# A hybrid gMLP, short-convolution and expert step on one core: mixing biases as products over 128 partitions, mixing between the last blocks of u, and a plan with a turn or two between an engine's step and its readers

## What is computed

```python
def chunk_mlp_mixer(x, w_in, ln_g, ln_b, w_s, b_s, w_out):
    z = jax.nn.gelu(x @ w_in)
    u, v = jnp.split(z, 2, axis=-1)
    v = layer_norm(v, ln_g, ln_b)
    ws = jnp.where(mask[None], w_s[:, :L, :L], 0).astype(v.dtype)
    bias = jnp.transpose(b_s[:, :L]).astype(v.dtype)
    mixed = jnp.einsum('gij,bcjgd->bcigd', ws, vc) + bias[None, None, :, :, None]
    y = (u * mixed.reshape(bsz, s_len, D_A)) @ w_out
    return y, v

def peer_ffn(h, w_query, sub_keys, expert_u, expert_v):
    ...
        u_sel = expert_u[idx]
        a = jax.nn.gelu(jnp.einsum('thkd,td->thk', u_sel, xb))
        return jnp.einsum('thk,thkd->td', g.astype(a.dtype) * a, expert_v[idx])
```

## Time and profile before

| | us |
|---|---|
| median of 3 runs | 1812.18 |
| lowest, highest of the 3 | 1812.14, 3855.36 |
| the profiled execution, its time | 1814.52 |
| its span in the profile | 1812.7 |

### The profile page before, as it was taken

How to read it: one execution, slowest core, us unless ns; L and a number is a source line. 1 busy time by engine, 2 the same in 40 slices (tenths; PEclk the granted TensorE clock), 3 DMA queues, 4 the chain that set the end, 5 groups by cost and what they waited for, 6 DMA issues and landing times.

```text
span 1812.7 us, 23002 instructions
## 1 busy us (share of the span) xinstructions
PE 1370.5 (76%) x8388; PEld 648.4 (36%) x8388; DVE 1217.0 (67%) x3197; ACT 293.1 (16%) x972; POOL 689.7 (38%) x580
## 2 busy tenths in 40 slices
PE   8997899998895887876664499779965667677643
PEld 6884345554462553541110066336511111111100
DVE  1237878545685867768889666666788975555565
ACT  1112123100222111211112111021211110000011
POOL 0003343323332343334544543343344444444453
PEclk9999799969997999986765599889977666665655
DMA  9739999979999999999999999999999999999996
GB/s 381 292 141 422 358 379 422 421 278 422 421 421 421 402 421 420 417 421 413 415 413 387 422 407 409 421 421 411 421 421 414 403 421 421 421 420 416 414 421 278
DMA packets 100657, 718.27 MB, mean 396 GB/s; under 512 B 12064, under 2 KB 12576, under 8 KB 13600
## 3 DMA queue, kind: packets, MB, share of 16 engines
q0 software_dynamic: 82944, 604.02, 81.1%
q1 hardware_dynamic: 17184, 112.19, 15.1%
q10 hardware_dynamic: 416, 0.60, 0.1%
HBM read 715.24 MB, written 1.52 MB: 395 GB/s over the span
## 4 chain that ended last, share of the span: by engine, by line
DMA 48%; PE 34%; DVE 8%; issue 7%; DVEq 2%; POOL 1%; ACT 0%; SPq 0%; POOLq 0%
DMA uvring<-expert_uv_dram,idx 44%; PE psum L657 13%; PE psum L668 10%; DMA wring<-w_chunks_dram 3%; PE psum L787 3%; PE psum L700 3%; DVE uvring L1198 2%; DVE diag L1209 1%; POOL uvring L610 1%; PE psum L770 1%; PE psum L767 1%; PE psum L676 1%; PE psum L649 1%; DVEq L990 1%; PE psum L739 1%
## 5 line engine op out<-in xcount | busy, mean ns | idle before, releaser
L610 POOL DMA_INDIRECT uvring<-expert_uv_dram,idx x576 | 689.5, 1197 | 1100.8 <-PE psum L657 874.5
L1198 DVE SCALAR_TENSOR_TENSOR uvring<-uvring,xn 128x1024 f32<-128x1024 f32 x576 | 705.1, 1224 | 371.7 <-DMA uvring<-expert_uv_dram,idx 360.4
L657 PE MATMUL psum<-uvring,diag 64*64 64x512 f32 x4096 | 704.8, 775 | 311.9 <-DVE diag L1209 300.5
L657 PEld LDWEIGHTS psum<-uvring,diag 64*64 64x64 f32 x4096 | 128.0, 155 | 734.4 <-DVE diag L1209 667.9
L914 ACT ACTIVATE a_gelu<-a_raw 128x1 f32<-128x1 f32 x576 | 115.2, 202 | 1109.9 <-DVE uvring L1198 1109.1
L668 PE MATMUL psum<-xT,wring 128*128 128x160 f32 (+1 forms) x1696 | 248.1, 302 | 15.4 <-DMA wring<-w_chunks_dram 14.7
L668 PEld LDWEIGHTS psum<-xT,wring 128*128 128x128 f32 x1696 | 226.9, 198 | 91.4 <-issue 61.9
L1209 DVE TENSOR_SCALAR diag<-twin,a_gelu,gate 128x64 f32<-128x64 f32 x512 | 158.9, 310 | 24.0 <-ACT a_gelu L914 23.8
L649 PE MATMUL psum<-uvring,diag 128*32 128x256 f32 x512 | 69.0, 634 | 90.5 <-DVE diag L1209 84.6
L836 ACT ACTIVATE arena<-psum 128x160 f32<-128x160 f32 (+2 forms) x160 | 47.7, 299 | 302.2 <-PE psum L668 240.9
L787 PE MATMUL psum<-wring,arena 128*128 128x256 f32 x288 | 70.0, 399 | 5.1 <-DMA wring<-w_chunks_dram 4.8
(11 more groups left out here) (117 smaller groups left out, 849.6 us busy)
## 6 DMA issues: line engine op xcount, KB each, us to landing
wring<-w_chunks_dram SPq DMA_DIRECT2D x73, 1024.0 KB
uvring<-w_chunks_dram SPq DMA_DIRECT2D x15, 1024.0 KB, 9.4
kept<-w_chunks_dram SPq DMA_DIRECT2D x12, 1024.0 KB, 15.6
uvring<-expert_uv_dram,idx POOLq DMA_INDIRECT x576
x<-x_tok_dram SPq DMA_DIRECT2D x2, 512.0 KB, 4.2
uvring<-ln_gain_dram SPq DMA_DIRECT2D x1, 1024.0 KB, 28.2
uvring<-ln_bias_dram SPq DMA_DIRECT2D x1, 1024.0 KB, 28.6
keys<-sub_keys_dram SPq DMA_DIRECT2D x2, 512.0 KB, 8.2
```

The costliest lines, as they stand in the source:

```text
L610: pool.indirect_dma_start(uvring[:, n % RING, :], None, expert_uv, bass.IndirectOffsetOnAxis(ap=idx[t][:, i:i + 1], axis=0),).then_inc(uv_ ...
L657: mm = nc.tensor.matmul(acc[64 * j:64 * j + 64, 512 * i:512 * (i + 1)], diag[64 * i:64 * i + 64, n % DIAGS, :], row[64 * i:64 * i + 64, D ...
L1198: nc.vector.scalar_tensor_tensor(out=uvring[:, slot, 0:D], in0=uvring[:, slot, 0:D], scalar=1.0, in1=xn[t][:, :], op0=ALU.mult, op1=ALU.mu ...
```

## The change

Three things are changed.

1. The bias of tiles 0 and 1 is a product over all 128 partitions, that of tile 2 still over 32. The biases of the 8 groups stand in the rows of `bias`, and the stationary matrix is column g of the unit matrix, repeated. The table loses a row, and the constant that is loaded for `bias` grows from 4 KB to 64 KB.
2. The mixing groups stand between the last blocks of u: group b-9 behind block b from block 9 on, the rest behind block 15. The `lnb` steps begin behind block 1 and not 3.
3. `ready` asks for distance in the plan: a step may read another engine's result one turn later, and for the kinds in `slow` TensorE's two turns later. The costs of TensorE's small steps are lower, those of the blocks higher, and TensorE's room in tile (0, 0) is 2.0 and not 1.85.

```diff
-    blk, row = KD * WIDTH[n] * mm, KD * WCOLS * mm
+    blk, row = 1.14 * KD * WIDTH[n] * mm, KD * WCOLS * mm
...
-            out.append(("PE", ("vq", c), row / 2, [x_read]))
+            out.append(("PE", ("vq", c), 0.6, [x_read]))
...
-            if n == 1 and 3 <= b < 11:
-                q, a = divmod(b - 3, 2)
-                out.append(("PE", ("lnb", q, a), 0.9, []))
+            if n == 1 and 1 <= b < 9:
+                q, a = divmod(b - 1, 2)
+                out.append(("PE", ("lnb", q, a), 0.6, []))
                 out.append(("DVE", ("lnrow", q, a), 1.4, [("lnb", q, a), ("root", "ln", 0, 2)]))
+
+            for g in range(GROUPS) if b == KA - 1 else (b - 9,) if b >= 9 else ():
+                if ("PE", ("mix", n, g)) in [step[:2] for step in out]:
+                    continue
+                out.append(("PE", ("mix", n, g), 1.0 + 0.8 * (n == 1), [("lnrow", 3, 1) if n else ("lnapply", 0, 1)]))
+                out.append(("DVE", ("gate", n, g), 0.5, [("mix", n, g), ("u read", n, 2 * g + 1)]))
...
-        for g in range(GROUPS):
-            out.append(("PE", ("mix", n, g), 1.0 + 0.8 * (n == 1), [("lnrow", 3, 1) if n else ("lnapply", 0, 1)]))
-            out.append(("DVE", ("gate", n, g), 0.5, [("mix", n, g), ("u read", n, 2 * g + 1)]))
...
-    (0, 0): {"DVE": 1.3, "ACT": 2.0, "PE": 1.85},
+    (0, 0): {"DVE": 1.3, "ACT": 2.0, "PE": 2.0},
...
-        same = ENGINES[:ENGINES.index(e) + 1]
-        if any(b not in turn or turn[b] > p or (turn[b] == p and by.get(b, "DVE") not in same) for b in behind):
+
+        slow = 2 if k[0] in ("v read", "vq read", "u read", "bch read", "q read", "gate", "add") else 1
+        lag = {who: 0 if who == e else slow if who == "PE" else 1 for who in ENGINES}
+        if any(b not in turn or turn[b] > p - (turn[b] >= 0) * lag[by.get(b, "DVE")] for b in behind):
             return False
...
-                        if t < 2:
-                            matrix, values = row_of(BIAS_ROW, slice(g * P, (g + 1) * P))
-                            bias = values.unsqueeze(1).to_broadcast([64, 2, P])
-                        else:
-
-                            matrix = ident[0:32, 0:1].to_broadcast([32, P])
-                            bias = bias4[:, g:g + 1, :].to_broadcast([32, 2 * SB, SS])
-                        nc.tensor.matmul(both[:, :, cols], matrix, bias, start=True, stop=False)
+
+                        values = (bias[:, :].unsqueeze(1).to_broadcast([P, 2, P]) if t < 2
+                                  else bias[0:32, 0:SS].unsqueeze(1).to_broadcast([32, 2 * SB, SS]))
+                        matrix = ident[0:r, g:g + 1].to_broadcast([r, P])
+                        nc.tensor.matmul(both[:, :, cols], matrix, values, start=True, stop=False)
```

More of the change, by code:

```diff
@@ L53 @@
 KEEP = 6
-GAIN_ROW, LN_ROW, BIAS_ROW = {("mix", 0): 0, ("ffn", 0): 1, ("mix", 1): 2, ("ffn", 1): 3, ("final", 1): 4}, 5, 9
+GAIN_ROW, LN_ROW = {("mix", 0): 0, ("ffn", 0): 1, ("mix", 1): 2, ("ffn", 1): 3, ("final", 1): 4}, 5
 RING = 7
@@ L130, in norm @@
         for j in range(2):
-            out.append(("PE", ("gb", which, l, tiles[0], j), 0.9, []))
+            out.append(("PE", ("gb", which, l, tiles[0], j), 0.6, []))
             out.append(("DVE", ("napply", which, l, tiles[0], j), 0.7 * len(tiles),
@@ L137, in transposed @@
             for j in range(2):
-                out.append(("PE", ("xT", l, which, t, j), 1.1, [("napply", which, l, tiles[0], j)]))
+                out.append(("PE", ("xT", l, which, t, j), 0.7, [("napply", which, l, tiles[0], j)]))
                 out.append(("ACT", ("xT read", l, which, t, j), 0.6, [("xT", l, which, t, j)]))
@@ L150, in mixer_steps @@
             if c % 2 == 0 and c:
-                out.append(("PE", ("vf", c // 2 - 1), 0.9, [("vq read", c // 2 - 1)]))
+                out.append(("PE", ("vf", c // 2 - 1), 0.6, [("vq read", c // 2 - 1)]))
                 out.append(("ACT", ("vf read", c // 2 - 1), 0.6, [("vf", c // 2 - 1)]))
-            out.append(("PE", ("vq", c), row / 2, [x_read]))
+            out.append(("PE", ("vq", c), 0.6, [x_read]))
             if c % 2:
@@ L195, in mixer_steps @@
             if 2 in tiles:
-                out.append(("PE", ("oq", l, c, h), row / 2, [gated]))
+                out.append(("PE", ("oq", l, c, h), 0.6, [gated]))
         out.append(("DVE", ("add", l, c, tiles[0]), 0.85, [("out", l, c, 1 - l, tiles[0])]))
@@ L210, in mixer_steps @@
             if b0 + count - 1 == b:
-                out.append(("PE", ("s", l, tiles[0], b0, count), 0.9, [("q read", n, b)]))
+                out.append(("PE", ("s", l, tiles[0], b0, count), 0.7, [("q read", n, b)]))
                 scanned = scanned_before(l, tiles[0], b0, count)
@@ L412, with trunk @@
 CHUNK_AFTER = plan_chunks()
-def trunk(nc, x_tok, w_chunks, rows, ln_gain, ln_bias, w_s, b_s4, conv_w, conv_state, sub_keys,
+def trunk(nc, x_tok, w_chunks, rows, ln_gain, ln_bias, w_s, b_s, conv_w, conv_state, sub_keys,
           expert_uv, ident_c, iota_c, fold_c, tril_c, smask_c,
@@ L436, in trunk @@
         ws2 = sb("ws2", [32, GROUPS, SS])
-        bias4 = sb("bias4", [32, GROUPS, SS])
+        bias = sb("bias", [P, P])
         wsm2 = sb("wsm2", [32, GROUPS, SB, SS])
@@ L576, in _ @@
                 (tril[:, :], tril_c), (smask[:, :, :], smask_c), (wsm[:, :, :], w_s),
-                (bias4[:, :, :], b_s4), (iota[:, :], iota_c), (fold[:, :], fold_c),
+                (bias[:, :], b_s), (iota[:, :], iota_c), (fold[:, :], fold_c),
                 (convw[:, :, :], conv_w), (state[:, :, :, :], conv_state),
@@ L1277 @@
                                 (norm_mix[0], norm_ffn[0], norm_mix[1], norm_ffn[1], norm_final,
-                                 a_ln_g, a_ln_b, a_b_s, np.zeros((64 - BIAS_ROW - 1, D), np.float32))]),
+                                 a_ln_g, a_ln_b, np.zeros((64 - LN_ROW - 4, D), np.float32))]),
         "ln_gain": np.asarray(a_ln_g),
@@ L1281 @@
         "w_s": np.asarray(a_w_s)[0].transpose(2, 0, 1),
-        "b_s4": np.concatenate([np.asarray(a_b_s).reshape(1, GROUPS, P)[:, :, 0:SS],
-                                np.zeros((31, GROUPS, SS), np.float32)]),
+        "b_s": np.concatenate([np.asarray(a_b_s).reshape(GROUPS, P), np.zeros((P - GROUPS, P), np.float32)]),
         "conv_w": np.asarray(b_conv_w)[0].reshape(3, KD, P).transpose(2, 0, 1),
```

## The result

The changed kernel took 1797.89 us (median of 4 runs, 1796.14 to 1798.35) beside 1812.18 for the kernel before (of its 4 runs beside these the one of 3855.36 is left out of the comparison): ratio 0.9919, 95% interval 0.9900 to 0.9939. By the 2% bound that is "same"; it is 14.3 us less, and the forecast was 15.2 less. The profiled execution took 1798.07 us with a span of 1796.3. It moved 718.33 MB, 0.06 more than before, as the larger constant says. At 421 GB/s that is 1706 us, so the DMA engines were idle for 90 us, where they were for 107.

What follows compares the result with a forecast made beforehand. The prediction took DMA to bound the kernel: 1706 us of transfers plus 107 us idle. Terms -3.1 - 13.7 + 3 - 2 = -15.8 us took the profiled 1814.52 to 1798.7, the median to 1796.4; it said 1797, range 1781 to 1815.

Steps and rivals of the forecast that it cites:

- within 2%: Whole kernel: the time differs from the kernel before by less than 2%, 36 us; chance 0.94.
- What bounds the kernel: Whole kernel: 718.27 MB at 421 GB/s, 1706 us, plus 107 us in which the DMA engines are idle.
- The prologue: Chain before the first gather: eight groups at 0.88 us in place of 1.27, 3.1 us less.
- The mixing of pass 1: 355 to 400 us: groups sharing turns with u blocks let DMA set the pace and close the gap, -13.7 us.
- As long as TensorE keeps 2.4 GHz: Mixing of pass 1: condition under which the DMA engines set the pace and the 15.2 us gap closes.
- The v stage: Pass 1, about 200 to 265 us: same products in 18 turns, not 22, leave more DMA idle, +3 us.
- the 13 to 16 us that the v stage was to show: Sign in the profile after: idle DMA between the v stage's first and last block, against 11.3 us measured before.
- The rest: Passes 2 and 3: thinner turns bring TensorE to the gather's pace in the first blocks, -2 us, between 0 and -5.
- TensorE at 1.2 GHz in turns 55 to 70: Rival, mixing of pass 1: the low clock stays despite the interleaving, slower at 1834 us; chance 0.07.
- The second rival: Query and bch passes: turns without a dense step let the clock fall, 21 us idle, 1817 us; chance 0.08.
- the 0.62 that spoke against the page: 355 to 400 us before: clock 0.62 with TensorE busy 44.73 of 45 us, cited against the skill's clock rule.
- The last rival: Waits worth more than work: v stage loses 4, mixing all 15.2, later passes 5, giving 1785 us; chance 0.12.

Runs made afterwards that it cites:

- e10: Kernel before with the new bias and the interleaving, but the old plan rule, costs and room; 1795.40 us, ratio 0.9907.
- e2: Kernel before with the interleaving alone (mixing groups between blocks of u, lnb steps earlier), old bias, old rule; 1798.96 us, ratio 0.9937.
- e4: Changed kernel without the interleaving: mixing groups back behind block 15, new bias and new plan rule kept; 1796.26 us, ratio 0.992.
- e3: Kernel before with the new plan rule, costs and room alone, old bias, groups behind the last u block; 1799.99 us, ratio 0.9953.
- e5: Changed kernel with the old bias products over 64 partitions and the old table; interleaving and new rule kept; 1797.48 us, ratio 0.9906.
- e1: Kernel before with the new bias products over 128 partitions alone, old plan and order; 1795.39 us, ratio 0.9912.
- e7: e1 with its bias product of tiles 0 and 1 over partitions 0 to 63 of the same new tile; 1813.54 us, ratio 0.9997.
- e9: e1 with tile 2's bias and mixing products in pass 1 also widened to 128 partitions by zero rows; 1795.91 us, ratio 0.9898.
- e8: Kernel before with two added products, which nobody reads, in each mixing group of pass 1; 1801.42 us, ratio 0.993.
- after_again: The changed kernel itself measured once more, on the same chip as e10 and e12; 1796.64 us, ratio 0.9913.
- e12: Products of e9 with the new plan rule, costs and room, mixing groups behind block 15; 1798.55 us, ratio 0.9923.

## Why the prediction was right, and where its reason was not

**The number.** 1797 said, 1797.89 measured. The range and the chance for "within 2%" held. No term is off by more than 1.3 us. In part that is luck: the largest term is the size of a gap that any of the three parts closes alone, so it came out right with a reason that was half wrong.

**What bounds the kernel.** Right. The sum by idle time of the DMA engines accounts for the result to 1 us. Summed in the same way, it leaves 1705 to 1707 us of the span in all thirteen traces, beside the 1706 that the prediction had from bytes and rate.

**The prologue, -3.1.** A group at 0.88 us as said; the window gives -3.6, and the first `dot` is at 133.2, in place of 136.9. That is the point which the prediction calls the first gather; the first one is issued at 127.6, before 131.1. With the new bias `out` starts at 78.4 to 79.9 us (seven traces), with the old one at 81.6 to 83.0 (six, of which that of the kernel before is the latest). So the term belongs to the bias; by the middle of each set it is 2.4 us, and the rest of the 3.6 is scatter between executions. The medians show it in two pairs (e10 under e2, e4 under e3) and not in the third (e5 beside the change).

**The mixing of pass 1, -13.7.** This is the step whose reason failed, with the size right (-14.3). It rested on two statements: that the interleaving closes the gap, and that the new bias is worth the 0.2 us of a change of partitions. The first is true (e2) but not needed, for the second is wrong: the bias alone closes it (e1), with groups in a row and without one block between. The prediction priced the pause at the high clock, where it is 0.2 us. The weight of the bias product lies elsewhere, in the clock. Two questions have to be kept apart there. One is whether it falls: it does behind waits for `diag` of 1.06 to 1.98 us at the first groups (before, e1, e7, e9), and it doesn't where no such wait is longer than 0.53 (e2, e3, e4, e5, e8, e10). Interleaving, the new rule and added work all shorten these waits. The other is whether it comes back: with the product over 64 partitions it doesn't until the groups are over (before, e7), with 128 it does within two groups (e1, e9). The medians go the same way: of the 37 runs of the kernel before and the 12 of e7 four are under 1803, of the six of e1 and the five of e9 all. So the gap was never TensorE's amount of work, which is 2.1 + 1.02 us in a turn, 0.6 above the gather's 2.49, but the clock at which it was done. Why 128 partitions bring it back, the shorter pause or the fuller product, stays open. "As long as TensorE keeps 2.4 GHz" stood as a condition of the sum; it was the whole term. The condition was also not quite met: the clock falls ahead of 364 us, behind the last group, and 0.9 us are lost.

**The v stage, +3.** -1.7 measured in its window and +3.4 in the next, so +1.7. The first block had the full clock, 3.72 us, which the prediction held for possible; with it the working's own figure is 13.4 - 11.3 = +2. That sets a sum beside a measured value: the same sum for the kernel before, 62.2 + 2.2 - 54.8, gives 9.6 idle and not 11.3. And the 13 to 16 us that the v stage was to show between its first and last block are not there: 355 GB/s from 201.3 to 262.8, which is 9.6 us. That TensorE would then be ahead of its weights, wait 4.50 us at the first block of u and take that block at the low clock wasn't foreseen; from 270 to 280 the DMA engines made 308 GB/s. The new rule does keep the clock here: the six traces with it (after, after_again, e3, e4, e5, e12) have the first v block at 3.72 to 4.00 us, and the seven with the old one (before, e1, e2, e7 to e10) at 5.0 to 5.8.

**The rest, -2.** -4.4 in the stretches that it spoke of (400 to 1060 and the first `bch` blocks, which have 421 now), and +3.1 behind them, which it didn't have. These and the 3.4 at the blocks of u go with the new rule: at the blocks of u its six traces lose 0.9 to 4.7 us and the other seven nothing, and behind the first `bch` blocks of pass 3 (from 1130 to 1760) 7.5 to 9.0 in place of 4.5 to 6.0.

**The rivals.** TensorE at 1.2 GHz in turns 55 to 70 didn't come, not even with the old bias (e2, e5). The second rival, empty turns that let the clock fall, is there on a small scale, ahead of `out` in pass 3 and not at the queries: 2.8 us and not 21, and the clock falls there with the old plan as well. The Trainium skill (TensorE: Matmul & The Clock Gate, Loop structure matters more than you think) says that long waits between bursts make the array run cold. The trace agrees in kind at this place, with 1.12 to 2.25 us between weighs and a clock of 0.50. The prediction was too quick to give it little weight: the 0.62 that spoke against the page was a stretch where the clock had first fallen behind such waits (0.93 and 1.18 us) and then stayed low under groups with the product over 64 partitions. The last rival, that waits are worth more than work, is in the first v block alone.

## What to carry to other kernels

Where an engine is "busy" all the time, look first at the clock it is granted, then at what the products are made of: here groups of small products, one of them over 64 partitions, stayed at half the clock once a wait had let it fall, and padding that product to 128 partitions, or shortening the waits (by the order, by the plan, even by added work), was faster. When several parts of a change touch one gap, each may close it alone; only the runs with one part each tell which, and the size of the sum says nothing on it. A kernel that mostly takes one time and rarely another by 14 us may stand at such an edge, and some ten runs show what three don't.

## What the runs showed of the hardware

- Products busy for 20.00 of 20 us were granted 0.50 of the clock with the bias product over 64 partitions (e7, 365 to 385). From 355 to 400 that kernel had 0.59, and 0.92 with the product over 128 (e1). The same groups with 64 partitions kept 1.00 where no wait had let the clock fall (e3, a turn of 3.07 us).
- At 2.4 GHz each change of the listed shape that was taken out of a turn of mixing took about 0.2 us with it: 3.07 us (e3), 2.87 (e1) and 2.68 (e9).
- All the falls looked at here came behind or among waits: for `diag` of 1.18 (before), 1.98 (e1), 1.06 (e7), 1.56 (e9), 3.21 and up to 2.25 us (after), for weights of 4.50 us. An `out` block that takes 3.72 us at 2.4 GHz took 5.51 and 5.56 behind such waits. Why waits like these don't let the clock fall in other places of the same traces is open.
- Why 3 of 12 runs of e3, 2 of 20 and 1 of 17 of the kernel before and 1 of 12 of e7 went the other way with the same instructions was not found out.
- The least time measured is that of e1 and e10, 1795.4 us; it isn't told apart from the changed kernel's 1796.64 to 1797.89.
